# Layers 1 and 2 of a hybrid backbone step: the norm's factor moved behind the projection, and mLSTM's second pass reordered

## The reference

```
h = rms_norm(x, g) * (1 + scale) + shift      # scale, shift, gate from silu(cond) @ w_mod; one set for
q, k, v, z = split(h @ w_in)                  # context tokens, one for latent tokens
x = x + gate * ((mixer(q, k, v) * silu(z)) @ w_out)
```

## Time and profile before

| | us |
|---|---|
| median of 3 runs | 2141.09 (2139.84 to 2141.14) |
| the profiled execution | 2136.39 |
| its span | 2134.6 |
| PE busy | 2006.7 (94%) |
| DVE busy | 1128.3 (53%) |
| ACT busy | 813.3 (38%) |
| POOL busy | 655.6 (31%) |
| mean granted clock of PE, share of full | 0.965 |

### The profile page before, as it was taken

One profiled execution on the slowest core, in us unless ns is written; L12 is line 12 of the kernel. 1 busy time (PEld: TensorE's weight loads), 2 busy tenths in 40 slices (PEclk: granted clock), 3 DMA queues, 4 the chain that ended last, 5 costly groups with the idle time before them and its releaser, 6 DMA issues.

```text
span 2134.6 us, 35884 instructions
## 1 busy us (share of the span) xinstructions
PE 2006.7 (94%) x14312; PEld 1744.1 (82%) x14312; DVE 1128.3 (53%) x2376; ACT 813.3 (38%) x1853; POOL 655.6 (31%) x884
## 2 busy tenths in 40 slices
PE   6999999989999997979989999999998989999997
PEld 4788888879999996969957868687788978888887
DVE  5476675664555554486544223252153365777764
ACT  5455564234444444031141232313222034565542
POOL 1333222543344322445410111101213643233232
PEclk7999999989999998989999999999999989999999
DMA  9212213422323223134322333324245222011111
GB/s 336 71 42 81 64 42 90 131 60 77 87 80 87 69 65 112 50 54 141 107 65 75 98 120 104 109 75 137 61 144 94 80 62 63 6 51 52 42 41 50
DMA packets 301812, 180.00 MB, mean 84 GB/s; under 512 B 59590, under 2 KB 276943, under 8 KB 301647
## 3 DMA queue, kind: packets, MB, share of 16 engines
q1 hardware_dynamic: 283908, 158.13, 25.7%
q10 hardware_dynamic: 17738, 19.59, 3.5%
HBM read 153.25 MB, written 24.43 MB: 83 GB/s over the span
## 4 chain that ended last, share of the span: by engine, by line
PE 80%; DVE 7%; ACT 7%; DMA 2%; issue 2%; SPq 1%; ACTq 0%; POOL 0%; DVEq 0%; POOLq 0%
PE pc L1752 22%; PE acc L1678 13%; PE acc L747 6%; PE acc L1874 4%; PE acc L1863 4%; PE pc L802 3%; PE pt L1885 3%; PE acc L737 3%; PE pt L747 3%; PE acc L2130 2%; PE acc L2118 2%; DMA out_mlstm_n<-amat 1%; PE acc L1706 1%; PE pt L2138 1%; PE pc L1777 1%
## 5 line engine op out<-in xcount | busy, mean ns | idle before, releaser
L1588 POOL TENSOR_TENSOR idle<-eps 128x1 f32<-128x1 f32 x146 | 41.9, 287 | 1413.3 <-PE pc L802 286.5
L1592 POOL TENSOR_TENSOR wl<-raw,wh 128x256 fp32r<-128x256 f32 x584 | 471.5, 837 | 11.7
L1752 PE MATMUL pc<-hh,wh 128*128 128x320 f32 x1152 | 379.5, 329 | 16.3 <-DVE hl L2801 8.0
L1752 PE MATMUL pc<-hl,wh 128*128 128x320 f32 x1152 | 361.9, 314 | 0.0
L1752 PE MATMUL pc<-hh,wl 128*128 128x320 f32 x1152 | 361.9, 314 | 0.0
L1752 PEld LDWEIGHTS pc<-hh,wh 128*128 128x128 f32 x1152 | 221.3, 192 | 28.1 <-issue 15.8
L1752 PEld LDWEIGHTS pc<-hl,wh 128*128 128x128 f32 x1152 | 222.5, 193 | 0.2 <-issue 0.2
L1752 PEld LDWEIGHTS pc<-hh,wl 128*128 128x128 f32 x1152 | 221.7, 192 | 0.0
L1589 POOL CAST wh<-raw 128x1024 fp32r<-128x1024 f32 x146 | 151.7, 1039 | 0.1
L2405 ACT COPY ht<-pt 128x512 f32<-128x512 f32 (+1 forms) x160 | 76.0, 526 | 190.7 <-PE pt L1885 190.6
L2905 DVE TENSOR_REDUCE gst<-acc 128x1 f32<-128x640 f32 (+1 forms) x160 | 113.3, 708 | 2.6 <-PE acc L1863 2.4
(11 more groups left out here) (412 smaller groups left out, 4472.7 us busy)
## 6 DMA issues: line engine op xcount, KB each, us to landing
raw<-in_w_mod SPq DMA_DIRECT2D x144, 256.0 KB, 3.4
raw<-in_gqa_w_in SPq DMA_DIRECT2D x80, 256.0 KB, 3.4
raw<-in_diff_w_in SPq DMA_DIRECT2D x64, 256.0 KB, 3.6
raw<-in_mlstm_w_in SPq DMA_DIRECT2D x64, 256.0 KB, 3.4
raw<-in_gqa_w_out SPq DMA_DIRECT2D x36, 256.0 KB, 3.3
praw<-in_w_mod SPq DMA_DIRECT2D x32, 256.0 KB, 9.6
out_mlstm_C<-amat ACTq DMA_DIRECT2D x16, 512.0 KB, 7.5
raw<-in_mlstm_w_out SPq DMA_DIRECT2D x32, 256.0 KB, 3.2
```

The costliest lines, as they stand in the source:

```text
L1592: ins = pool.tensor_tensor(wl[:, s, k:k + 2], raw[:, r, k:k + 2], wh[:, s, k:k + 2].bitcast(F32), ALU.subtract)
L1752: ins = pe.matmul(pc[:, c:c + 320], w[:, sl, kt, :], h[:, kt, t:t + 320], start=kt == 0 and n == 0, stop=kt == KT - 1 and n == 2)
```

## The change

**Layers 1 and 2, input.** x·(1+scale)·g is rounded to hh without the factor 1/rms, k-tile by k-tile as each output panel of the layer before is gated into x: ACT makes hh and the square (rounded), DVE adds the squares (added) and makes hl (u_low). hh and hl get two more columns in front that hold the shift for context and latent tokens (shift_low), so half 0 is now 322 columns (the two, and tokens 0 to 319), half 1 stays at 320. PE runs the first unit at once: total 0 is issued after four k-tiles, total 1 after the unit. Behind the projection DVE multiplies each PSUM half by rinv and copies the two shift columns to a small tile; ACT adds them as a bias. In layer 1 every unit goes this way (DVE evac, then ACT evac); in layer 2 each x_m panel (DVE multiplies in place in PSUM, ACT copies with bias) and each gate half (in place, then ACT's silu with bias). The layers 0 and 3 stay as they are.

**Layer 2's start.** m_begin is counted at the first gated panel of layer 1's output; DVE makes the first bd before the second reciprocal; bdt is copied by ACT, its second group from pc. POOL's wait for h_ready at its third split of layer 1 goes.

**Second pass.** k's four blocks are copied by DVE in passes 1 to 3; ACT's weights then run without copies between. PE waits for a_made and mv_copied not ahead of the steps but inside step 0, behind its products with C; ahead of them it waits for d_full. ACT copies a direction's four state tiles first and issues its six DMAs after them (state_out); both gates of block 0, then states, then normal. DVE has a tile t1 of its own for the steps. In the last pass the output panel 1 stands ahead of the turns, and turns 2 and 3 behind state 1.

The core of the diff:

```diff
@@ PE, layer 1: units
+                    for kt in range(KT):
+                        if u == 0 and kt in ARRIVED:
+                            pe.wait_ge(*seen(h_ready, ARRIVED[kt]))
+                        if u == 0 and kt == 4:
+                            totals_open[0](0)
+                        if u == 1 and kt == KT - 1:
+                            pe.wait_ge(*seen(h_ready))
+                        for n, (w, h) in enumerate(((wh, hh), (wh, hl), (wl, hh))):
+                            ins = pe.matmul(pc[:, o:o + c1 - c0], w[:, slot[0], kt, :], h[:, kt, c0:c1],
+                                            start=kt == 0 and n == 0, stop=kt == KT - 1 and n == 2)
@@ PE, second pass
                 pe.wait_ge(*qk_count(p, 2 * MB - 1))
-                pe.wait_ge(qk_moved, len(MOVED))
+                    if s == 0:
+                        pe.wait_ge(a_made, 2 * QT * (p + 1))
+                        pe.wait_ge(mv_copied, 3 * (p + 1))
...
-                pe.wait_ge(a_made, 2 * QT * (p + 1))
-                pe.wait_ge(mv_copied, 3 * (p + 1))
+                pe.wait_ge(d_full, 2 * QT * (p + 1))
...
                     out_panel(0, 0)
                     state(p, 0)
-                    turned(p, 0, 1, 2, 3)
                     out_panel(0, 1)
+                    turned(p, 0, 1)
                     state(p, 1)
+                    turned(p, 2, 3)
@@ ACT: hh and squares while the output projection runs
+                def high(kt, *parts):
+                    for a0, a1, g in parts:
+                        ins = act.activation(hh[:, kt, 2 + a0:2 + a1], x[:, kt, a0:a1], ACT.Copy, scale=amul[:, kt, g:g + 1])
+                    ins.then_inc(ht_full, 1)
+                for kt in order[0:KT - 1]:
+                    act.wait_ge(*seen(x_ready))
+                    if kinds[layer] == "mlstm" and kt == order[0]:
...
+                        act.copy(flag[:, :], eps[:, 0:1]).then_inc(m_begin, 1)
+                    high(kt, (0, P, 0), (P, T, 1))
+                    act.activation(SQUARES[order.index(kt)], x[:, kt, :], ACT.Square).then_inc(xr_used, 1)
@@ DVE, layer 1: evacuation
+                    dve.wait_ge(*seen(unit_done[half]))
+                    if half == 0:
+                        dve.tensor_scalar(bcol[:, kind, :], pc[:, 0:2], SM if kind == 0 else 1.0, None, ALU.mult)
+                    dve.tensor_tensor(d[:, t:t + 320], pc[:, c:c + 320], rinv[:, t:t + 320], ALU.mult).then_inc(c_free[half], 1)
@@ DVE, layer 2: first pass
-            dve.wait_ge(m_in, 16 * 10)
+            dve.wait_ge(m_begin, 1)
...
+            dve.wait_ge(m_in, 16 * 10)
+            bds(0)
+            second_root()
...
+                    dve.wait_ge(*seen(proj_done[blk % 2]))
+                    dve.tensor_copy(mcol[:, blk % 2, :], acc[b][:, AO - 2:AO])
+                    dve.tensor_tensor(acc[b][:, AO:AO + T], acc[b][:, AO:AO + T], rinv[:, :], ALU.mult).then_inc(xr_full, 1)
@@ DVE, gates of layer 2
+                if half == 0:
+                    dve.tensor_copy(mcol[:, 2 + blk % 2, :], pc[:, 0:2])
+                dve.tensor_tensor(pc[:, c:c + 320], pc[:, c:c + 320], rinv[:, t:t + 320], ALU.mult).then_inc(xr_full, 1)
@@ DVE, last panel and the new hl
+                for a0, a1, g in parts:
+                    ins = dve.scalar_tensor_tensor(out=hl[:, kt, 2 + a0:2 + a1], in0=x[:, kt, a0:a1], scalar=amul[:, kt, g:g + 1],
+                                                   in1=hh[:, kt, 2 + a0:2 + a1].bitcast(F32), op0=ALU.mult, op1=ALU.subtract)
@@ ACT, second pass
+                state(p, 0)
+                state_out(p, 0)
                 normal(p)
...
+                state(p, 1)
+                state_out(p, 1)
@@ POOL
-                        if i == 2:
-                            pool.wait_ge(h_ready, 2 * KT * (layer + 1))
```

More of the change, by code:

```diff
@@ L1401, in mlstm_dve @@
                     bds(ORDER[p + 1])
+                else:
+                    for blk in range(MB):
+                        for half in range(2):
+                            gate(p, blk, half)
                 for s in range(NST):
@@ L1411, in mlstm_dve @@
                     out(0, 0, RING[(p, "o", 0)])
+                    out(0, 1, RING[(p, "o", 1)])
+                else:
+                    for blk in range(MB):
+                        for half in range(2 if blk < MB - 1 else 1):
+                            gate(p, blk, half)
                 gated(p)
-            out(0, 1, RING[(MH - 1, "o", 1)])
             turn.k = start + len(RING)
@@ L1722, in last_panel, with total @@
                     return bs
-                for t, c in halves():
+                def total(half):
+                    t, c = halves()[half]
                     pe.wait_ge(*seen(sq_full))
                     pe.matmul(acc[bs][:, c:c + 320], ones, two[:, 1, t:t + 320], start=False, stop=True).then_inc(acc_full[bs], 1)
+                if deferred:
+                    totals_open.append(total)
+                else:
+                    total(0)
+                    total(1)
             pe.wait_ge(ident_in, 16)
@@ L2323, in roots, with rounded @@
                     act.activation(rinv[:, t:t + 320], acc[b][:, c:c + 320], ACT.Sqrt, bias=eps[:, 0:1], scale=1.0 / D).then_inc(root_ready, 1)
+            def rounded(layer):
+                mod, amul = mods[layer % 2], amuls[layer % 2]
+                order = LAST_ORDER if kinds[layer - 1] == "gqa" else list(range(KT))
+                act.wait_ge(*seen(mod_ready))
+                act.copy(hh[:, :, 0:2], mod[:, 0:KT, :])
+                def high(kt, *parts):
[5 more added lines that the diff above has]
+                    if kinds[layer] == "mlstm" and kt == order[0]:
+                        seen.back(act, "vtm0")
+                        seen.back(act, "kp")
+                        act.copy(flag[:, :], eps[:, 0:1]).then_inc(m_begin, 1)
+                    high(kt, (0, P, 0), (P, T, 1))
+                    act.activation(SQUARES[order.index(kt)], x[:, kt, :], ACT.Square).then_inc(xr_used, 1)
+                seen(xr_used, KT - 1)
+                act.activation(warm_col[:, :], eps[:, 0:1], ACT.Sqrt)
+                act.wait_ge(*seen(xr_full))
+                high(KT - 1, *PARTS[0])
+                b, full = use()
+                act.wait_ge(*full)
+                for half, (t, c) in enumerate(halves()):
+                    act.activation(rinv[:, t:t + 320], acc[b][:, c:c + 320], ACT.Sqrt, bias=eps[:, 0:1], scale=1.0 / D).then_inc(root_ready, 1)
+                    if half == 0:
+                        act.wait_ge(*seen(x_ready))
+                        high(KT - 1, *PARTS[1])
+                        act.wait_ge(*seen(acc_full[b]))
             def modulate(layer):
@@ L2643, in _ @@
                     gqa_layer(layer)
+                    for half in range(2):
+                        seen(c_free[half], 5 * GQ_KV)
                 else:
@@ L2828, in normalise @@
                 seen(h_ready, 4)
+                seen(xr_full, 2 * KT)
+                seen(xr_used, sum(PLAIN[half](kt) for half in range(2) for kt in range(KT)))
             def minus(out, a, high):
@@ L3096, in diff_layer @@
                         output(n - 1)
+                    if qt == 4 and not last:
+                        gate(NU * (h + 1) + 6)
+                    if qt == 0 and h:
+                        gate(NU * h + 7)
                     if qt == 1 and h:
@@ L3170, in _ @@
                     gqa_layer(layer)
+                    for half in range(2):
+                        seen(unit_done[half], 5 * GQ_KV)
                 else:
```

409 lines of the change are left out of this document (262 added, 147 removed).

## The result

The changed kernel took 2116.24 us (median of four runs, 2110.68 to 2119.70) where the kernel before took 2141.11 beside it: 0.9879 of it, 95% interval 0.9859 to 0.9900. In a later set of runs the two stood at 2112.63 and 2140.06, 0.9878 [0.9859, 0.9898]. So 25 to 26 us are gone, where 47 were forecast.

The account below looks back on a forecast made before the run. PE was taken to bound the kernel, with gains to come from its stops. Terms of 50.9 us off and 3.5 on gave 47.4 less than the median of 2141.09, say 2094 us; range 2083 to 2112.

Parts of the forecast that it names:

- Parts 1 and 2: Starts of layers 1 and 2: projection runs straight on, norm's factor applied behind it; gains 15.2 and 19.9 us.
- The 0.9 us that DVE would be late at the first head: Layer 2's start: DVE needs 16.2 us before the first block against PE's 15.3, cutting the gain to 19.9.
- rival A: DVE becomes the bound at the starts and in parts of layer 1, slowed beside POOL's splits: 2110 us, chance 0.23.
- the sign: Projection passes of 322 columns would stay within 1 ns, if the forecast was right.
- the 0.9 forecast: In-place PSUM multiplication stands on PE's path at xm_gates of the last head, adding 0.9 us.
- Parts 3 and 4: Second pass: DVE copies k in passes 1 to 3, 8.4 us; waits moved behind step 0's C products, 3.1.
- Part 5: Second pass, states stored later: PE's stop only moves to state 1, 0 taken; bounds +1.5 to -9.0 us.
- Part 6: Last pass's new order: state 0 through the last turns takes 20.6 us instead of 24.9, gain 4.3.
- Term (a): Projection half 0 has 322 columns for 320, shifted start taken as free: 1.4 us added.
- rival C: Shifted moving operand slows all 3072 projection passes; at 0.02 us each 61 us on, 2155; chance 0.04.
- its first place: The two starts: u_low and bd products slowed beside POOL's splits, in-place form at double, 8 us.
- Rival A's second place: Layer 1's 40 iterations: 0.2 us lost in each, another 8 us.

Follow-up runs that it names:

- w45: Changed kernel with SyncE loading output panels (0,4) and (0,5) ahead of the wait for turned blocks and the third y load, last pass: 2109.4 us, ratio 0.9846.
- pad2: Kernel before with rows of hh, hl and hlf 642 columns long, all passes still 320 wide: ratio 1.0026, 5.6 us more.
- off2: Kernel before with tiles hh, hl and hlf begun two columns (8 bytes) later, rows still 640: ratio 1.0034, 7 us more.
- the stage experiment: Changed kernel with VectorE gating next panels before working off the last and ScalarE squaring before rounding, output stages of layers 0 and 1: 2121.06 us, 0.9883.
- the first experiment: The same run as w45: 2109.4 us, ratio 0.9846.

## Why the prediction was wrong, step by step

**Parts 1 and 2, right.** 15.1 for 15.2 and 21.1 for 19.9. PE has no idle time at either start of the projection (0.7 us later for ACT's copy of bdt) and the clock stays at 1.00. The 0.9 us that DVE would be late at the first head did not come, because its bd products took 2.52 us instead of 5.55. In the kernel before, POOL was splitting weights beside them, after the change for a smaller share (4.39 us busy of 5.60, and 0.99 of 2.70; the windows in the columns of the earlier trace rows):

```profile
938.70:944.30 5.60, 5.60 (x40) 5.60 (x39) 5.57 (x13) 0.76 (x2) 4.39 (x6) 1.00 0.00 0
```

```profile
913.40:916.10 2.70, 2.70 (x20) 2.70 (x19) 2.67 (x14) 0.00 (x0) 0.99 (x2) 1.00 0.00 0
```

So the 5.5 us in the working held the price of rival A already. The in-place multiplication took 0.82, the value taken. In layer 1 a pass of 322 columns takes 147.5 ns for 146.5, within the 1 ns that was to be the sign. The stop at xm_gates (L677, L623) rose from 0.9 to 2.1, by 1.2 for the 0.9 forecast.

**Parts 3 and 4, near.** The three passes gave 9.4 with part 5 in it, for 8.9. Of the stops at k's last block and S, 1.21 and 2.08 in each of three passes or 9.9, there stay 3.4 for DVE's copy of the last block: 6.5 gained where 8.4 were forecast. Of part 4's 3.1, the 1.0 in pass 0 and 1.4 in passes 1 and 2 came; in pass 3 PE stood 1.3 ahead of the gate units and steps and now stands 1.4, mostly for ACT's last gate. What made up for it is 1.0 at the states and 1.1 us in which PE was busy less, because the clock was low for 3 us there and not for 7; that last gain is no merit of the working. What part 3 is worth by time inside the changed kernel, 15 us, holds for its order of ACT and includes the clock; the stops alone are 8.1.

**Part 5, a size off.** Taken as 0, with 9.0 as the far bound. Against the kernel before, the working came out: the stop at state 0 is gone and the one at state 1 is 2.36, 2.02 and 2.85 us, where the two together were 2.85, 2.66 and 2.70. Against the changed kernel without part 5 it is worth 4.4 us in the passes. There PE stands 11.0 at the states and 1.9 at a gate; the term of 0 was worked out from the stops of the kernel before, which are shorter. Why they are longer beside the other parts is open.

**Part 6, the step that failed most: -4.3 forecast, +9.5 measured.** The working counted PE's pieces and one wait each for normal and the stores. It said nothing of SP, whose loads of panels (0,4) and on, and of y, are queued behind a wait for the turned blocks. Moving panel (0,1) and state 1 ahead of the last turns took 13 us, their stops with them, from behind that wait. In numbers: 8.5 of stop for weights and some 2.8 of low clock behind it (w45 gives back 7 by time, 10.1 in the stretch), 3.8 before the second turns where 0.5 was allowed (the store of state 0, issued at 1579.57, took 13.23 us to land, and PE had work until 1589.8), 0.6 before the first where 1.0 was allowed. The stops alone are 12.9 against the 1.5 of waits in the sum; the whole miss is 13.8 us.

**Term (a), mis-sized: 1.4 forecast.** The working took the row of fp32 passes as proof that a shifted start is free. pad2 and off2 give 5.6 and 7.3 us, and the pace is slower in all layers that read hh, the unchanged 0 and 3 too; rival C named this mechanism, but at 0.02 us a pass, some fifteen times the 0.0013 that 7.10 for 7.04 a panel gives. By the passes it is 960 at 1.4 ns more in each of layers 0 and 3, or 1.3 us, and 1536 at 1.5 in layer 1, or 2.2: that is all of the +1.3, most of the +2.9 and less than half of the +3.2. Another 0.9 of the +3.2 lies in the prologue, on DVE and ACT just ahead of layer 0's projection (53.17 for 52.29 in the chain); why is open, and so is the last 1.0.

**The output stages, a term missing.** They were costed as covered. The chain of layer 0's shows how they weren't: DVE's sum of squares waits 1.78 us for ACT at each single panel, and DVE serves panels in order. Beside POOL's splits four of u_low take 3.09 us, without them 1.94:

```profile
430.54 3.09 DVE L3318 SCALAR_TENSOR_TENSOR hl<-x,amul,hh 128x128 fp32r<-128x128 f32 x4
...
436.33 0.83 DVE L3307 TENSOR_TENSOR two<-two 128x640 f32<-128x640 f32 x1 [1.78 <-ACT two L2453]
437.20 1.94 DVE L3318 SCALAR_TENSOR_TENSOR hl<-x,amul,hh 128x128 fp32r<-128x128 f32 x4
```

This is the price of rival A at its first place, which was left at 0 in the sum. How much of the 4.7 us in the two stages is this price, and how much the order of the queues (2.5 of stop, as the stage experiment shows), is not shown: no run took POOL's splits away. POOL was busy 2.38 of 3.2 us in the first stretch and 0.31 of 2.0 in the second. The Trainium skill (GPSIMD Engine Reference, 1. Specifications) names DVE instructions with two SBUF inputs as those in contention with GpSimd. u_low is one, and so are the bd products above; the evacuations, with one input in PSUM, kept to 0.47 to 0.49 us in all 64 cases, as it would have it. Rival A's second place, layer 1's iterations, did not cost: no stop of PE there waits for an evacuation.

Of the 21.7 us by which the sum was off, 13.8 are the order of the last pass, 5.8 the projections of layers 0, 1 and 3 beyond the forecast 0.7 (some 4 of it the slower passes), 4.7 the output stages and 0.9 the prologue; the starts and the passes of layer 2 gave 3.5 more than forecast. That 2116 is near rival A's 2110 is luck: most of the miss lies in part 6, where A puts nothing.

## What to carry to other kernels

When work is moved on one engine, ask of each queue not only what it waits for, but what its waits now stand behind: an order that shortens PE's own sequence can take the cover from a load that waits in another queue for the result of a later step. Prices of an address change can't be taken from instructions of another type; the cheapest test is the unchanged kernel with the tile moved and nothing else. And a short stop may cost twice, once as a stop and once in the clock behind it, so changes around PE's stops are to be judged by time and by busy time for the same instructions.

## What the runs showed of the hardware

- A 320-column pass (fp32 stored in the rounded type) takes between 145.8 and 147.7 ns at full clock in layer 1 depending on where its moving operand begins and how long its rows are (7.00 to 7.09 us for 48); weights begun 8 bytes later alone change nothing (7.04). Over some 5000 passes the two ends would be some 10 us apart, by this estimate.
- The granted clock also falls below 1.00 in stretches where PE hardly stands: the same stretch of layer 2's first pass took 157.0 us in the changed kernel and 163.2 in the first experiment, whose code there is the same, and a window of 27 us with PE busy 26.55 had a clock of 0.94 there:

```profile
927.00:954.00 27.00, 26.55 (x176) 25.87 (x180) 18.37 (x34) 8.96 (x17) 13.43 (x18) 0.94 0.29 96
```

  Differences of 3 to 6 us between two single executions can be no effect of the code, so single profiles here were compared stretch by stretch.
- DVE multiplies in place in PSUM at the price of a copy out of it: 640 columns 0.82 us, as the copy; 320 columns 0.49 to 0.50, where the form that reads PSUM and writes SBUF takes 0.48.
- DVE instructions with two SBUF inputs take longer while POOL splits weights: twelve bd products 5.55 us with POOL busy 4.39 of 5.60, 2.52 with POOL busy 0.99 of 2.70.
